# Prompt attention steps moved in between the last five preparation steps, and the turned probabilities copied ahead of the exponentials

## The reference

```python
def attend_block(qb, qpos_b, k, v, kpos):
    s = jnp.einsum('bqhe,bkhe->bhqk', qb, k, preferred_element_type=jnp.float32) * (QK_HEAD ** -0.5)
    vis = (kpos[None, :] // CHUNK) <= (qpos_b[:, None] // CHUNK)
    s = jnp.where(vis[None, None], s, NEG_INF)
    p = jax.nn.softmax(s, axis=-1)
    return jnp.einsum('bhqk,bkhd->bqhd', p.astype(v.dtype), v)

# in each layer
q = (rms_norm(q_lat, p['g_q_lora']) @ p['w_q_up']).reshape(B, S, N_HEADS, QK_HEAD)
q = concat([rms_norm(q[..., :QK_NOPE], g_qn), apply_rope(rms_norm(q[..., QK_NOPE:], g_qr), cos, sin)])
kv = (ckv_all @ p['w_kv_up']).reshape(B, T, N_HEADS, QK_NOPE + V_HEAD)
k = concat([rms_norm(kv[..., :QK_NOPE], g_kn), k_rope shared by the heads]); v = kv[..., QK_NOPE:]
o_att = block_causal_attention(q, k, v, qpos, kpos)      # query blocks of 128, chunk mask of 64
```

## Time and profile before

| what | value |
|---|---|
| median of 3 executions | 1438.18 us (1423.65, 1438.18, 1445.41) |
| the profiled execution, its own time | 1430.43 us |
| its span in the trace | 1428.6 us |
| TensorE's mean granted clock | 0.98 of 2.4 GHz |

### The profile page before, as it was taken

The page is one execution under the profiler, slowest core; times in us unless marked ns, Lnnn a source line. Parts: engine busy times, 40 slices in busy tenths (PEclk is TensorE's granted clock), DMA queues, the critical chain, the costliest instruction groups (busy, mean ns, idle before and its releaser), DMA issues.

```text
span 1428.6 us, 25408 instructions
## 1 busy us (share of the span) xinstructions
PE 1356.5 (95%) x9448; PEld 1246.0 (87%) x9448; DVE 950.2 (67%) x1526; ACT 586.7 (41%) x953; POOL 867.7 (61%) x460
## 2 busy tenths in 40 slices
PE   6998989998999999999999989899899999999998
PEld 6885656898999999999998656679899999999997
DVE  3456577587676766666736586756976767676765
ACT  4335467344333333333332455653443333333331
POOL 3645057276777777777654434454677777777771
PEclk8999999999999999999999999879999999999999
DMA  7110021131222222333412000221222222222221
GB/s 227 60 38 11 5 60 29 32 89 58 91 89 88 88 88 89 93 95 95 138 60 65 14 4 1 59 60 30 60 89 89 89 88 88 88 88 88 88 88 67
DMA packets 138577, 102.35 MB, mean 72 GB/s; under 512 B 8972, under 2 KB 125136, under 8 KB 138512
## 3 DMA queue, kind: packets, MB, share of 16 engines
q1 hardware_dynamic: 135848, 100.46, 23.3%
q10 hardware_dynamic: 2664, 1.02, 0.3%
HBM read 98.10 MB, written 3.36 MB: 71 GB/s over the span
## 4 chain that ended last, share of the span: by engine, by line
PE 80%; DVE 13%; issue 2%; ACT 2%; POOL 2%; DMA 1%; ACTq 0%; SPq 0%; DVEq 0%
PE ps L2207 33%; PE ps L1915 8%; PE ps L1919 8%; PE ps L1916 8%; PE ps L1860 3%; PE ps L1898 3%; PE ps L1900 3%; PE ps L1899 3%; PE ps L2148 3%; PE ps L2128 3%; POOL rs L752 2%; DVE hs_lo L1305 2%; PE ps L2012 2%; PE ps L2105 1%; DVE tm L1457 1%
## 5 line engine op out<-in xcount | busy, mean ns | idle before, releaser
L752 POOL TENSOR_TENSOR rs<-ms,mhalf 128x8 f32<-128x8 f32 (+5 forms) x66 | 140.1, 2124 | 212.1 <-DVE ms L1435 78.6
L851 POOL TENSOR_TENSOR w_lo<-raw,w_hi 128x1024 fp32r<-128x1024 f32 x132 | 228.6, 1758 | 43.9 <-ACT w_hi L1256 39.7
L1689 DVE TENSOR_REDUCE raw<-raw 128x512 f32<-128x1024 f32 x184 | 230.8, 1255 | 0.4
L851 POOL TENSOR_TENSOR w_lo_a<-raw,w_hi_a 128x512 fp32r<-128x512 f32 x88 | 180.9, 2067 | 74.7 <-ACT w_hi_a L1256 70.1
L1915 PE MATMUL ps<-act_hi,w_hi 128*128 128x288 f32 x704 | 195.9, 293 | 3.5 <-issue 3.5
L1916 PE MATMUL ps<-act_lo,w_hi 128*128 128x288 f32 x704 | 196.1, 294 | 0.0
L1651 DVE TENSOR_TENSOR xT<-ps,xT 128x576 f32<-128x576 f32 x192 | 142.5, 752 | 38.5 <-PE ps L1919 38.4
L2207 PE MATMUL ps<-t_hi,w_hi 128*128 128x288 f32 x528 | 157.6, 299 | 6.3 <-DVE side L1714 5.2
L2207 PE MATMUL ps<-t_lo,w_hi 128*128 128x288 f32 x528 | 156.7, 297 | 0.0
L2207 PE MATMUL ps<-t_hi,w_lo 128*128 128x288 f32 x528 | 156.5, 296 | 0.0
L1919 PE MATMUL ps<-act_hi,w_lo 128*128 128x288 f32 x704 | 150.5, 295 | 0.0
(11 more groups left out here) (243 smaller groups left out, 3512.1 us busy)
## 6 DMA issues: line engine op xcount, KB each, us to landing
raw<-in_w_gate SPq DMA_DIRECT2D x88, 256.0 KB, 3.7
raw<-in_w_up SPq DMA_DIRECT2D x88, 256.0 KB, 3.7
raw<-in_w_down SPq DMA_DIRECT2D x20, 1024.0 KB, 4.8
raw<-in_w_in SPq DMA_DIRECT2D x10, 1024.0 KB, 5.5
raw<-in_w_o SPq DMA_DIRECT2D x16, 512.0 KB, 5.4
x_tm<-in_x_prompt SPq DMA_DIRECT2D x4, 512.0 KB, 5.1
raw<-in_w_down SPq DMA_DIRECT2D x8, 256.0 KB, 3.7
out_y_prompt<-x_tm SPq DMA_DIRECT2D x8, 256.0 KB, 2.2
```

The source lines that it names most:

```text
L752: pool.tensor_tensor(rs[:, c:c + n], ms[:, c:c + n], mhalf[:, 0:n], ALU.pow).then_inc(rs_ready, 1)
L851: pool.tensor_tensor(lo[:, k, cols], src, hi[:, k, cols].bitcast(F32), ALU.subtract).then_inc(lo_split, 1)
L1689: dve.tensor_reduce(raw[:, 2, j * Q:(j + 1) * Q], added(a, b), AX.X, ALU.add).then_inc(sums_added, 1)
```

## The change

It has two parts. The first replaces both hand-written orders. Before, attention steps 0, 1 and 2 stood after preparation steps 6, 7 and 8 on TensorE; now step 0 stands right behind preparation step 4, and steps 0 to 4 alternate with the preparation steps 5 to 9. The lists of the readers run one preparation step later than TensorE's, as before. The second part is on ScalarE: in each attention step, the copy of the turned probabilities of step n-2 stands before the exponentials of step n, not behind them. The explicit wait for the transposes of step n-2 that stood before the exponentials goes, since `prompt_pt` now makes the same wait.

```diff
 PREP, ATTEND = [("prep", n) for n in range(len(P_TILES) + 2)], [("attend", n) for n in range(len(P_STEPS) + 3)]
-P_ORDER = PREP[2:7] + [ATTEND[0], PREP[7], ATTEND[1], PREP[8], ATTEND[2], PREP[9]] + ATTEND[3:]
-P_ORDER_READERS = PREP[2:7] + [PREP[7], ATTEND[0], PREP[8], ATTEND[1], PREP[9], ATTEND[2]] + ATTEND[3:]
-assert P_ORDER[-len(P_STEPS) - 1] == ("prep", len(P_TILES) + 1)
+EARLY_STEPS = 5
+P_ORDER = PREP[2:5] + [x for n in range(EARLY_STEPS) for x in (ATTEND[n], PREP[n + 5])] + ATTEND[EARLY_STEPS:]
+P_ORDER_READERS = (PREP[2:6] + [x for n in range(EARLY_STEPS - 1) for x in (ATTEND[n], PREP[n + 6])]
+                   + ATTEND[EARLY_STEPS - 1:])
...
                     if what == "prep":
                         preps_run(L["p_preps"], [n])
                         continue
+                    if 2 <= n < len(P_STEPS) + 2:
+                        prompt_pt(n - 2)
                     if n < len(P_STEPS):
                         i, _, nh = P_STEPS[n]
                         u = L["p_steps"][n]["s"]
                         act.wait_ge(nm_ready, STEPS * l + HEAD_PAIRS + n + 1)
-                        if n >= 2:
-                            filled(act, L["p_steps"][n - 2]["t"])
...
                         ins.then_inc(S["s_exp"], 1)
-                    if 2 <= n < len(P_STEPS) + 2:
-                        prompt_pt(n - 2)
```

More of the change, by code:

```diff
@@ L224 @@
 PREP, ATTEND = [("prep", n) for n in range(len(P_TILES) + 2)], [("attend", n) for n in range(len(P_STEPS) + 3)]
-P_ORDER = PREP[2:7] + [ATTEND[0], PREP[7], ATTEND[1], PREP[8], ATTEND[2], PREP[9]] + ATTEND[3:]
-P_ORDER_READERS = PREP[2:7] + [PREP[7], ATTEND[0], PREP[8], ATTEND[1], PREP[9], ATTEND[2]] + ATTEND[3:]
-assert P_ORDER[-len(P_STEPS) - 1] == ("prep", len(P_TILES) + 1)
+EARLY_STEPS = 5
+P_ORDER = PREP[2:5] + [x for n in range(EARLY_STEPS) for x in (ATTEND[n], PREP[n + 5])] + ATTEND[EARLY_STEPS:]
+P_ORDER_READERS = (PREP[2:6] + [x for n in range(EARLY_STEPS - 1) for x in (ATTEND[n], PREP[n + 6])]
+                   + ATTEND[EARLY_STEPS - 1:])
+assert sorted(P_ORDER) == sorted(P_ORDER_READERS) == sorted(PREP[2:] + ATTEND)
 O_PARTS = [(PT_ * WIDTH, HEAD_PAIRS)] + [(i * WIDTH, HEADS) for i in range(PT_)]
@@ L235 @@
 APPLIED = {"o0": 9, "o1": 13, "o2": 15, "o3": 21}
-assert list(SQUARED) == list(ASKED) and min(SQUARED.values()) > 3
+assert list(SQUARED) == list(ASKED) and min(SQUARED.values()) >= EARLY_STEPS - 1
 W_O_HIGH = (13, 15)
```

## The result

The changed kernel took 1456.99 us in the median of four executions (1443.25 to 1457.23), the kernel before 1431.45 (1423.65 to 1445.41). The ratio is 1.0156, with a 95% interval from 1.0095 to 1.0216: about 22 us slower. The interval reaches past 2%, so it is settled that the kernel is slower, and not settled whether by more or less than 2%. The ratios leave out executions that took over 1.5% longer than the fastest of the same kernel, so they are not the quotients of the medians printed beside them. The profiled execution took 1457.06 us with a span of 1455.3, 26.7 above the one before.

What follows compares the result with a forecast made beforehand. TensorE, busy 95% of the span, its waits and its granted clock were taken as the bound. Order +13.0, copies -5.0 and clock +4.0 gave +12 us on 1434.4, so 1446 us; own range 1438 to 1456, whole range 1431 to 1463.

Steps and rivals of the forecast that it cites:

- step 1: First layer's prompt attention: TensorE's scores of step 0 wait 5.0 us for VectorE's copy of k0, a new wait.
- steps 3 to 5: Later in that stretch: TensorE idles 2.9 us before k1's transposes, 4.0 before scores 2, 2.1 before step 0's outputs.
- The clock: Half clock behind TensorE's new idle time in the preparation: 2.0 us per layer, 4.0 added; bounds 0 and 7.
- part one: New order of attention and preparation steps: scores 6 start 6.5 us late per layer, 13.0 in both; bounds 2.8, 8.6.
- Part two: ScalarE's copies ahead of exponentials: TensorE waits less for turned probabilities, minus 2.5 us per layer, minus 5.0 in all.
- C: Early scores fill TensorE's old gaps in both layers' preparation; with the copies minus 18.6 us, 1416 us; chance 0.05.
- D: No change at all, 1434 us: TensorE's waits only change names; chance 0.05.
- A: Faster: second layer's long half-clock stretch goes with its wait for `pT`; 1431.7 us, 6 under the median; chance 0.10.
- B: Much slower: thin stretch wholly at half clock, both layers keep it through block 2's steps; 1463 us; chance 0.12.

Runs made afterwards that it cites:

- part two alone: Kernel before with only ScalarE's copies of turned probabilities put ahead of the exponentials, old order of steps kept: 1422.44 us, ratio 0.9937 against the kernel before.

## Why the prediction was right, and where it was short

The forecast was slower by 12 us and 1446 us; measured were some 22 us slower by the ratio, 26.7 between the two profiled executions, and 1457 us. So the direction and the causes named were right, and the size was about half of what came. The time lies in the range of 1431 to 1463 us but one us above the forecast's own 1438 to 1456. That narrower range was not the sum of the bounds either: with 2.8 to 8.6, -3.4 to 0 per layer and 0 to 14 for the clock they reach from 1433 to 1466.

**The wait for k0 (step 1) was right**: 5.0 us forecast, 5.09 measured in both layers, released by VectorE's copy of k0. Moving that copy ahead took it away, so its cause is shown and not only read.

**The chain of waits (steps 3 to 5) was right almost to the tenth**: 2.9, 4.0 and 2.1 us forecast, 2.91, 3.87 and 2.45 measured, by the releasers named. The idle time of P came out at 14.4, where the waits forecast add up to 14.0. What the part had wrong is its end: scores 6 came 12.2 late, not 6.5, mainly because instructions behind the waits ran at half clock.

**The clock was the term mis-sized.** I put it at 2.0 per layer on top of part one, near the one dip of the old trace, with bounds of 0 and 7. What is missing beside part one is 12.2 - 6.5 = 5.7 per layer, and the rows give 5.3 of it to the clock. In the run of part two alone, the same instructions of P stand in the first layer at full clock (us, busy, granted clock, DMA share, GB/s):

```profile
187.40:214.60 27.20, 21.86 (x136) 1.00 0.30 78
```

They are busy for 21.86 us there and for 27.15 in the changed kernel; the other 0.4 is the idle time above. Kept busy, TensorE came to P = 37.7, where my schedule at full clock has 29.4 + 6.5 = 35.9; the rest is the dip behind the wait that stayed unfilled. I had counted four idle pieces and priced one dip. There are three, of 1.6 to 1.9 us each by the rows' lengths, and they fall on q3's and k3's projections and what stands beside them. They were on the path: the next waits did not get shorter by them (2.91 us with q3's projection at 3.49 or at 2.75).

**Part two was named rightly and mis-sized in both directions.** I gave it 2.5 per layer, in S. With the weight block out of the way S takes 36.8 instead of 40.1, so 3.3. In the mixed stretch the new order without it takes 3.7 more of P, which I had not seen, because I laid out the new order with the new place of the copies only and never asked what the old place would have cost there. How much of that the copies save is not shown: 1.45 of it stands ahead of the first of them. What I missed on the other side is the 1.9 us weight block, which stands behind the exponentials of step 13 and so now directly ahead of the copy in step 14, with a wait of 1.51 us (0.89 before) where I wrote that copies wait only for their own transposes. Behind it the half clock fell in both layers. In the profiled executions S rose by 4.5 and fell by 2.3, against a forecast of -2.5 each. Where the long stretch falls differs from execution to execution, so how near the total came is partly luck.

**The rivals.** C, early scores fill the old gaps, fell as argued: they wait for k0 themselves. D fell with it. A has half of the truth in the wrong kernel: the long stretches do go with the waits for `pT`, but only once the weight block is halved, and not with this change. B was nearest in kind. Its half clock was there in both layers of S, and in part of P.

## What to carry to other kernels

A step moved forward doesn't only need its inputs computed, it needs them copied out, and on an engine that works its list in order the copy may stand behind the wait of a later tile; look at what stands ahead of the releaser, and move that first. Price the half clock behind new idle time on TensorE piece by piece, here 1.6 to 1.9 us for each of three dips, because it falls on work that the path runs through. When a copy is put ahead of something, ask which long instruction now stands ahead of it.

## What the runs showed of the hardware that I had not expected

Filling three waits with 12 useless matmuls per layer made the kernel 8.5 us faster by its lowest time, with clock 1.00 instead of 0.58 to 0.72 around them. And the kernel before spreads over 26 us in one core's runs, while the two old-order kernels with halved weight blocks stay within 4 over four executions each, and the two new-order ones within 7 over ten, with S at the same 36.8 us in both layers of each profiled execution. The kernel before's mean granted clock goes with its time: 0.986 to 0.988 in its runs near 1424 us, 0.975 to 0.977 near 1437 and 0.966 to 0.967 near 1449. So most of this kernel's noise is how much half clock an execution happens to get.
